# One decoder layer on one core: a projection product cut in three, a transpose moved behind three matmuls, and PSUM bank pairs exchanged

## The chip, the cores and the metric

The kernel runs on one core of a Trainium2 chip. The metric is the device time of one execution in microseconds (us), lower is better. The core has five engines, each with a queue of its own that it works through in order: PE (TensorE, matmuls and transposes), ACT (ScalarE), DVE (VectorE), POOL (GpSimd) and SP (SyncE, which here issues nearly all DMAs). They wait for each other through semaphores.

## The reference, cut to what matters

One layer of a decoder block for 256 tokens of width 1024, all in float32:

```python
z = rmsnorm(x, g_mix) @ w_in                       # 1024 -> 5184 columns
nq, nkv, ngate, dq, dk, dv, iq, ik, iw, ga, gb = split_cols(z, IN_SPLITS)
o_a = nsa_mixer(nq, nkv, ngate, ...)               # compressed, selected and window branch
o_b = dsa_mixer(dq, dk, dv, iq, ik, iw, ...)       # indexer keeps 64 keys of a query
merged = sigmoid(ga) * (o_a @ w_branch_a) + sigmoid(gb) * (o_b @ w_branch_b)
x = x + merged @ w_out
x = x + moe_ffn(rmsnorm(x, g_ffn), ...)            # top 4 of 32 experts, 12 MB of weights each
x = x + sigmoid(rmsnorm(x, g_ple) @ w_ple_gate) * (p @ w_ple)
```

The compressed branch of the first mixer pools windows of 32 raw keys and values:

```python
zb = z[:, cmp_tok] + pe                            # raw keys or values plus a position table
hdn = silu(einsum('bclgd,lde->bcge', zb, w1))
```

## The kernel before, in words

Every engine has a hand-written program. In order of time there are three parts.

**Front.** `ORDER` lists the first stages. `Z0` to `Z6` are the first seven of eleven products of x with a block of columns of `w_in` (`CHUNKS`, at most 512 columns). A product has 8 matmuls (over the 8 row tiles of the weight, `KT`) for each of 2 token tiles `t`. In program text a matmul of float32 is one instruction; in the trace it is two records, so a row with x16 is 8 matmuls. Product c goes to PSUM banks `ps[2*(c%2)+t]`. ACT copies a finished tile into `z` (line 769), scaled by the norm, and counts `z_ev` up; PE counts `z_ps` up when a tile is done. The stages `T:...` are transposes: PE writes one of the banks ps4 and ps5 in turn, ACT copies it out and counts `t_ev`, and the job after next may only start when that bank is copied (`tbank`). `T:K0`, `T:K1` (lines 1286, 1287) are the keys of the selected and the window branch, `T:R0`, `T:R1` (line 1291) the raw keys and values of the compressed branch for each token tile, `T:PE` (line 1295) the position table. After `T:PE` is copied, DVE adds the position table in eight instructions (line 1005, `zb`) and counts `zb_ready`. Product 6 (`Z6`) is the value block of the second mixer, which nothing reads until the first `values` step. POOL adds the mask to the bias (line 667, `Bd`) once `T:R1` is there.

**Attention.** 24 units of two heads (`UNITS`) are worked through in 28 steps. At step u PE does `scores(u)` (line 1372), a special stage if the step has one, `flip(u-3)` (the transposes of the probabilities, line 1380), some matmuls of the four remaining products of `w_in` (`late`, line 1408; 3 a step at first, into banks ps0 and ps1) and `values(u-4)` (lines 1395, 1399). The special stage of step 1 is `HID` (line 1353), the first matmuls of the compressed branch, which wait for `zb_ready`. At step 11 (`C_AFTER`) PE also does `T:C0` and `T:C1` (line 1309), transposes of the compressed branch's probabilities. DVE works on the logits (lines 1065, 1076), ACT does exponentials (783) and copies: probabilities (792), outputs (800), late products (809).

**After attention.** `branch(i)` (line 1439) multiplies the mixers' outputs with `w_branch_a` and `w_branch_b`, two banks for each i. Before `branch(0)` PE waits for `ld_wab`, for all outputs (`o_ev`) and for the copies of all late products (`z_ev`). Then come merged rows, `w_out` (line 1460), the norm, the router and its ranks, and the experts: `visit` for each of 32 experts, with line 369 for the first weights. A visit takes six pieces of 2 MB, in a ring of nine slots.

**DMA.** SP's queue is in order. It loads product c's weights into one of four buffers (`WBUF`) when the product before in this buffer is done (`z_ps`). The first five expert pieces are issued after `o_ev`, two after the fourth `branch` (`pr_ps`), one after `wo_ps` 4, one after `hp_ready`, and each one from then on when PE has used the piece in its slot (`pieces_used`; lines 313 and 315).

Of the kernel before, what the change touches and what calls it, by code (L numbers as in the profile page):

```python
# [18 lines left out]
ALU = mybir.AluOpType  # L19
# [39 lines left out]


ORDER = ["T:G", "T:X0", "T:X1", "T:X2", "T:X3", "Z0", "ER", "Z1", "T:IX0", "T:IX1", "Z2", "I", "T:DQ0", "T:DQ1", "Z3",
         "T:DK0", "T:DK1", "Z4", "T:NQ0", "T:NQ1", "Z5", "Z6", "T:K0", "T:K1", "T:R0", "T:R1", "T:PE"]

UNITS = [("dsa", t, j) for t in (0, 1) for j in range(4)] + [(b, t, j) for t in (0, 1) for j in range(4) for b in ("slc", "win")]
NU = len(UNITS)
# [3 lines left out]
STAGE_AT = {1: "HID", 5: "CMPKV", 7: "T:KC", 8: "T:CS"}  # L69
HIDDEN_AT, KEYS_AT, NORMED_AT, C_SOFT = 3, 5, 6, 9  # L70
C_AFTER = 8


TJOBS = [x for x in ORDER if x.startswith("T:")]
# [24 lines left out]
def block_kernel(nc, io, out):  # L99
    ctx = ExitStack()  # L100
    with ctx:
# [425 lines left out]
        with nc.Block() as block:  # L527
# [160 lines left out]
            def _(sc):  # L688
# [66 lines left out]
                for stage in ORDER:  # L755
                    if stage.startswith("T:"):
                        tjob(stage)
                    elif stage == "ER":
                        sc.wait_ge(er_ps, 1)
                        a.copy(erow, ps[6][0:16, 0:384]).then_inc(er_sb, 1)  # L760
                    elif stage[0] == "Z":
                        c = int(stage[1:])
                        o, n = CHUNKS[c]
                        for t in range(TT):
                            sc.wait_ge(z_ps, 2 * c + t + 1)
                            src = ps[2 * (c % 2) + t][:, 0:n]
                            if c == 0 and t == 0:
                                sc.wait_ge(x_rs, 1)
                            a.activation(z[:, t, o:o + n], src, ACT.Copy, scale=rs[:, t:t + 1]).then_inc(z_ev, 1)
                        if c == C_N2:  # L770
                            sc.wait_ge(z_ev, 2 * c + 2)
                            a.activation(gsig, z[:, :, O_NG:O_NG + 24], ACT.Sigmoid)
                    elif stage == "I":
                        for i in range(6):
                            sc.wait_ge(i_ps, i + 1)
                            if i >= 2:
                                sc.wait_ge(i_used, i - 1)
                            a.activation(rl[:, i % 2, :], ps[7 - i % 2][:, :], ACT.Relu).then_inc(i_rl, 1)
# [124 lines left out]
            def _(ve):  # L903
# [207 lines left out]
                for i in range(4):  # L1111
                    t, n = i // 2, (i % 2) * 512
                    ve.wait_ge(pr_ps, i + 1)
                    ve.wait_ge(gates_ready, t + 1)
                    ch(d.tensor_tensor(mtmp[:, 0, :], ps[2 * (i % 2)][:, :], gates[:, t, n:n + 512], ALU.mult))
                    ch(d.tensor_tensor(mtmp[:, 1, :], ps[2 * (i % 2) + 1][:, :], gates[:, t, DM + n:DM + n + 512], ALU.mult))
                    d.tensor_tensor(merged[:, t, n:n + 512], mtmp[:, 0, :], mtmp[:, 1, :], ALU.add).then_inc(pr_used, 1)
                    ve.wait_ge(pr_used, i + 1)
                ve.wait_ge(ld_consts, 16)
# [14 lines left out]
                def add(i):  # L1134
                    t, c = i // 2, slice((i % 2) * 512, (i % 2 + 1) * 512)
                    ve.wait_ge(wo_ps, i + 1)
                    d.tensor_tensor(x[:, t, c], ps[i][:, :], x[:, t, c], ALU.add).then_inc(x2_ready, 1)

                def square(i):

# [111 lines left out]
            def _(te):  # L1252
# [59 lines left out]
                for stage in ORDER:  # L1312
                    if stage.startswith("T:"):
                        tjob(stage)
                    elif stage[0] == "Z":
                        c = int(stage[1:])
                        o, n = CHUNKS[c]
                        te.wait_ge(ld_w[WBUF[c]], 16 * WBUF[0:c + 1].count(WBUF[c]))
                        if c >= 2:
                            te.wait_ge(z_ev, 2 * (c - 1))  # L1320
                        wv = wbuf[:, WBUF[c] * 4096:WBUF[c] * 4096 + KT * n].rearrange("p (k n) -> p k n", k=KT)
                        for t in range(TT):
                            for k in range(KT):
                                if c == 0 and t == 0 and k % 2 == 0:
                                    te.wait_ge(t_ev, 2 + k // 2)
                                l = mm(ps[2 * (c % 2) + t][:, 0:n], hTv[:, k, t * P:(t + 1) * P], wv[:, k, :], start=k == 0, stop=k == KT - 1)  # L1326
                            l.then_inc(z_ps, 1)
                    elif stage == "ER":
                        te.wait_ge(ld_tab, 48)
                        mm(ps[6][0:16, 0:384], tab, onehot, start=True, stop=True).then_inc(er_ps, 1)  # L1330
# [82 lines left out]
                for u in range(STEPS):  # L1413
# [4 lines left out]
                    if 3 <= u < NU + 3:  # L1418
                        flip(u - 3)
                        if u - 3 == C_AFTER:  # L1420
                            tjob("T:C0")
                            tjob("T:C1")
                    for step in LATE_OF[u]:
                        late(*step)
                    if u >= 4:
                        values(u - 4)


                te.wait_ge(ld_wab, 48)
                te.wait_ge(o_ev, NITEM)  # L1430
                te.wait_ge(z_ev, 2 * NZ)

                def branch(i):
                    t, n = i // 2, (i % 2) * 512
                    if i >= 2:
                        te.wait_ge(pr_used, i - 1)
                    for m_ in range(2):
                        for j in range(4):
                            l = mm(ps[2 * (i % 2) + m_][:, :], oTv[:, m_, j, t * P:(t + 1) * P], (wa, wb)[m_][:, j, n:n + 512], start=j == 0, stop=j == 3)  # L1439
                    l.then_inc(pr_ps, 1)  # L1440

                def half_rows(src, n, at, cols):
# [11 lines left out]
                def w_out(i, ks=range(KT)):  # L1454
# [2 lines left out]
                        te.wait_ge(t_ev, NT + 2 * t + 2)  # L1457
                        te.wait_ge(pr_used, 3 + t)
                    for k in ks:
                        l = mm(ps[i][:, :], hTv[:, k, t * P:(t + 1) * P], wo[:, k, n:n + 512], start=k == 0, stop=k == KT - 1)  # L1460
                    if ks[-1] == KT - 1:
                        l.then_inc(wo_ps, 1)

# [115 lines left out]
```

## Time and profile before

| | |
|---|---|
| time, median of 3 runs (lowest, highest) | 1246.31 us (1244.42, 1247.02) |
| time of the profiled execution | 1244.73 us |
| its span in the trace | 1242.8 us |
| PE busy | 1143.1 us (92%) |
| DVE, ACT, POOL busy | 273.6, 188.1, 35.6 us |
| mean DMA rate | 361 GB/s, 448.29 MB |
| start of `branch(0)` | 219.11 us |
| start of the first expert matmul | 289.64 us |

Times in the trace start at the span's start. A row of an engine gives start, duration and instruction, and in brackets how long the engine stood idle before it and what released it. A matmul's duration holds its way through the array, so the starts of neighbouring rows, and not the sum of durations, tell how long a piece of PE's program takes.

### The profile page before, as it was taken

How to read it: one execution, taken by the hardware profiler on the slowest of the kernel's cores; microseconds unless marked ns; L12 is line 12 of the kernel's file. 1: busy time of each engine (PE TensorE's matmuls, PEld its weight loads, DVE VectorE, ACT ScalarE, POOL GpSimd, SP SyncE). 2: the span in 40 equal slices, each digit the busy share in tenths (PEclk: the TensorE clock that was granted, in tenths of full speed). 3: DMA queues.
4: the chain of work that ended last, by engine and by line, in shares of the span. 5: the costliest groups of instructions: out<-in, count | busy, mean ns of one | idle time of the engine just before them, and what ended most of it. 6: DMA issues, size and time to landing. Idle time of an engine off the chain costs nothing.

```text
span 1242.8 us, 15211 instructions
## 1 busy us (share of the span) xinstructions
PE 1143.1 (92%) x6372; PEld 475.9 (38%) x6372; DVE 273.6 (22%) x786; ACT 188.1 (15%) x405; POOL 35.6 (3%) x49
## 2 busy tenths in 40 slices
PE   7998999998999999998899888888888888888878
PEld 4454544454333343333333333333333333333334
DVE  1473534254111121111111111111111111111122
ACT  2223434222111111111100000000000000000010
POOL 2121100000000000000000000000000000000000
PEclk9999999998999999999999999999999999999999
DMA  8935050969999999999999999999999999999980
GB/s 275 331 136 175 28 136 1 402 234 352 429 426 427 429 428 428 428 429 428 425 426 427 429 428 429 428 428 429 429 428 428 430 429 428 427 429 429 427 341 34
DMA packets 51626, 448.29 MB, mean 361 GB/s; under 512 B 9298, under 2 KB 12215, under 8 KB 26919
## 3 DMA queue, kind: packets, MB, share of 16 engines
q1 hardware_dynamic: 49998, 441.67, 85.8%
q0 software_dynamic: 1264, 5.27, 1.2%
q10 hardware_dynamic: 328, 0.86, 0.3%
q8 instruction: 25, 0.41, 0.1%
q14 instruction: 11, 0.08, 0.0%
HBM read 446.71 MB, written 4.22 MB: 363 GB/s over the span
## 4 chain that ended last, share of the span: by engine, by line
PE 59%; DMA 37%; ACT 2%; DVE 1%; issue 1%; ACTq 0%; POOL 0%; DVEq 0%; POOLq 0%
DMA ring<-in_w_e 24%; PE ps L369 16%; DMA wbuf<-in_w_e 13%; PE ps L396 11%; PE ps L1326 7%; PE ps L1408 4%; PE ps L347 3%; PE ps L338 2%; PE ps L1525 2%; PE ps L1439 2%; PE ps L1460 2%; PE ps L1372 2%; ACT wbuf L460 1%; PE ps L386 1%; PE ps L1399 1%; PE ps L361 1%
## 5 line engine op out<-in xcount | busy, mean ns | idle before, releaser
L369 PE MATMUL ps<-ring,wbuf 128*64 128x512 f32 x1392 | 312.7, 596 | 35.0 <-DMA ring<-in_w_e 34.7
L369 PEld LDWEIGHTS ps<-ring,wbuf 128*64 128x64 f32 x1392 | 96.5, 137 | 238.9 <-issue 162.2
L507 DVE TENSOR_SCALAR oT<-ps 128x512 f32<-128x512 f32 x32 | 22.1, 692 | 737.0 <-PE ps L369 737.0
L369 PE MATMUL ps<-wbuf 128*64 128x512 f32 x656 | 147.8, 595 | 17.5 <-DMA wbuf<-in_w_e 17.4
L396 PE MATMUL ps<-ring,wbuf 128*64 128x512 f32 x672 | 149.5, 595 | 14.2 <-ACT wbuf L460 14.2
L456 ACT ACTIVATE oT<-oT 128x512 f32<-128x512 f32 x32 | 20.1, 630 | 510.5 <-DVE oT L507 510.5
L369 PEld LDWEIGHTS ps<-wbuf 128*64 128x64 f32 x656 | 45.1, 136 | 113.3 <-issue 75.4
L1326 PE MATMUL ps<-wbuf,hT 128*128 128x512 f32 (+2 forms) x224 | 86.5, 545 | 0.0
L396 PEld LDWEIGHTS ps<-ring,wbuf 128*64 128x64 f32 x672 | 46.4, 137 | 102.1 <-issue 83.9
L396 PE MATMUL ps<-wbuf 128*64 128x512 f32 x352 | 78.6, 595 | 7.4 <-ACT wbuf L460 7.4
L347 PE MATMUL ps<-wbuf 64*128 64x512 f32 x264 | 65.6, 615 | 0.7 <-ACT wbuf L462 0.7
L1408 PE MATMUL ps<-wbuf,hT 128*128 128x512 f32 x128 | 59.8, 594 | 0.0
L1326 PEld LDWEIGHTS ps<-wbuf,hT 128*128 128x128 f32 x224 | 42.9, 194 | 40.2 <-issue 37.1
L338 PE MATMUL ps<-misc,gat 128*128 128x64 bf16 x1584 | 53.7, 193 | 1.7 <-DVE gat L1161 1.7
L338 PEld LDWEIGHTS ps<-misc,gat 128*128 128x128 bf16 x1584 | 52.8, 98 | 2.1 <-DVE misc L1196 1.7
L462 ACT COPY wbuf<-ps 128x512 f32<-128x512 f32 x32 | 18.8, 586 | 230.0 <-PE ps L396 230.0
L396 PEld LDWEIGHTS ps<-wbuf 128*64 128x64 f32 x352 | 24.3, 137 | 53.5 <-issue 44.0
L347 PEld LDWEIGHTS ps<-wbuf 64*128 64x128 f32 x264 | 22.7, 186 | 43.1 <-issue 41.5
L487 DVE TENSOR_TENSOR wbuf<-ps,misc 128x512 f32<-128x512 f32 x33 | 22.8, 692 | 28.6 <-PE ps L338 28.6
L1408 PEld LDWEIGHTS ps<-wbuf,hT 128*128 128x128 f32 x128 | 22.3, 190 | 17.5 <-issue 17.4
L1439 PE MATMUL ps<-wbuf,oT 128*128 128x512 f32 x64 | 27.9, 593 | 1.0 <-ACT gat L809 1.0
L1460 PE MATMUL ps<-wbuf,hT 128*128 128x512 f32 x64 | 28.5, 594 | 0.0
(237 smaller groups left out, 762.0 us busy)
## 6 DMA issues: line engine op xcount, KB each, us to landing
ring<-in_w_e SPq DMA_DIRECT2D x129, 2048.0 KB, 38.0
wbuf<-in_w_e SPq DMA_DIRECT2D x63, 2048.0 KB, 38.1
wbuf<-in_w_in SPq DMA_DIRECT2D x9, 2048.0 KB, 9.2
wbuf<-in_w_out SPq DMA_DIRECT2D x1, 4096.0 KB, 14.0
rel_rows_repeated<-rel_rows POOLq DMA_DIRECT2D x1, 3072.0 KB, 19.6
ring<-rel_rows_repeated POOLq DMA_DIRECT2D x1, 2048.0 KB, 12.0
wbuf<-in_w_branch_a SPq DMA_DIRECT2D x2, 1024.0 KB, 10.0
wbuf<-in_w_branch_b SPq DMA_DIRECT2D x1, 2048.0 KB, 17.9
```

Source lines behind the costliest of these rows:

```text
L338: l = mm(O[:, k * SLOTS:(k + 1) * SLOTS], hp[:, q, t, rows_of(k)], S[:, t, :], start=t == 0 and q == 0, stop=t == TT - 1 and q == 2)
L347: l = mm(ps[4 + 2 * t + n][:, :], wST[h, t * P:(t + 1) * P], oe[h, :], start=start, stop=False, skip_group_check=True)
L369: l = mm((G, Lb)[n // 2][(n % 2) * SLOTS:(n % 2 + 1) * SLOTS, :], xeT[:, k, :], slots[at][:, r * 2 * DFF + n * 512:r * 2 * DFF + (n + 1) * ...
L396: l = mm(O[n * SLOTS:(n + 1) * SLOTS, :], actT[:, r, h * SLOTS:(h + 1) * SLOTS], slots[at][:, r * DM + n * 512:r * DM + (n + 1) * 512], st ...
L487: d.tensor_tensor(xeT, ps[2][:, :].rearrange("p (k c) -> p k c", k=KT), bc(gT[:, 16:24], SLOTS), ALU.mult).then_inc(s["xe_ready"], 1)
L507: d.tensor_scalar(gc, ps[0][:, :], LIMIT, None, ALU.min).then_inc(s["gc_ready"], 1)
L1326: l = mm(ps[2 * (c % 2) + t][:, 0:n], hTv[:, k, t * P:(t + 1) * P], wv[:, k, :], start=k == 0, stop=k == KT - 1)
L1372: mm(ps[2 + u % 2][:, 0:2 * n], q[:, j, t * P:(t + 1) * P], k[:, :, 0:n], start=True, stop=True).then_inc(s_ps, 1)
L1408: l = mm(ps[t][:, :], hTv[:, k, t * P:(t + 1) * P], wbuf[:, WBUF[c] * 4096 + k * 512:WBUF[c] * 4096 + (k + 1) * 512], start=k == 0, stop=k ...
L1439: l = mm(ps[2 * (i % 2) + m_][:, :], oTv[:, m_, j, t * P:(t + 1) * P], (wa, wb)[m_][:, j, n:n + 512], start=j == 0, stop=j == 3)
L1460: l = mm(ps[i][:, :], hTv[:, k, t * P:(t + 1) * P], wo[:, k, n:n + 512], start=k == 0, stop=k == KT - 1)
L1525: l = mm(ps[4 + i % 4][:, 0:w_], x3T[:, k, t * P:(t + 1) * P], wple_g[k // 4][:, k % 4, n:n + w_], start=k == 0, stop=k == KT - 1)
```

## The change

`Z6` is cut in three in `ORDER`: token tile 0 whole, then after `T:K0` and `T:K1` the first four matmuls of tile 1, and after `T:PE` its last four. The new function `product` reads these names. `T:C1` moves on PE from directly behind `T:C0` to behind the three late matmuls of its step; ACT's order is unchanged there. The four `branch` products and the four `w_out` products trade the bank pairs ps0, ps1 and ps2, ps3, and the wait for the last late copy moves from `branch(0)` to `branch(1)`.

```diff
 ORDER = [...
-         "T:DK0", "T:DK1", "Z4", "T:NQ0", "T:NQ1", "Z5", "Z6", "T:K0", "T:K1", "T:R0", "T:R1", "T:PE"]
+         "T:DK0", "T:DK1", "Z4", "T:NQ0", "T:NQ1", "Z5", "Z6 0 0:8", "T:K0", "T:K1", "Z6 1 0:4", "T:R0", "T:R1", "T:PE", "Z6 1 4:8"]
+def product(stage):
+    c, *part = stage[1:].split()
+    if not part:
+        return int(c), [(t, range(KT)) for t in range(TT)]
+    lo, hi = (int(k) for k in part[1].split(":"))
+    return int(c), [(int(part[0]), range(lo, hi))]
...
-                        for t in range(TT):
+                        for t in [t for t, ks in parts if ks[-1] == KT - 1]:
                             sc.wait_ge(z_ps, 2 * c + t + 1)
...
-                    ch(d.tensor_tensor(mtmp[:, 0, :], ps[2 * (i % 2)][:, :], gates[:, t, n:n + 512], ALU.mult))
+                    ch(d.tensor_tensor(mtmp[:, 0, :], ps[2 - 2 * (i % 2)][:, :], gates[:, t, n:n + 512], ALU.mult))
-                    d.tensor_tensor(x[:, t, c], ps[i][:, :], x[:, t, c], ALU.add).then_inc(x2_ready, 1)
+                    d.tensor_tensor(x[:, t, c], ps[(i + 2) % 4][:, :], x[:, t, c], ALU.add).then_inc(x2_ready, 1)
...
-                        for t in range(TT):
-                            for k in range(KT):
+                        for t, ks in parts:
+                            for k in ks:
...
                         if u - 3 == C_AFTER:
                             tjob("T:C0")
-                            tjob("T:C1")
                     for step in LATE_OF[u]:
                         late(*step)
+                    if u - 3 == C_AFTER:
+                        tjob("T:C1")
...
                 te.wait_ge(o_ev, NITEM)
-                te.wait_ge(z_ev, 2 * NZ)
                 def branch(i):
                     t, n = i // 2, (i % 2) * 512
+                    if i == 1:
+                        te.wait_ge(z_ev, 2 * NZ)
```

The order of PE's program around product 6, before. `ps` is a PSUM bank, line 1326 a product of `w_in`, 1286 and 1287 `T:K`, 1291 `T:R`, 1295 `T:PE`, 1372 the first scores; an x behind a row counts instructions.

```order
L1326 MATMUL ps<-wbuf,hT 128x512 [waits z_ev,ld_w0]
L1326 MATMUL ps<-wbuf,hT 128x512 x15
L1286 MATMUL ps<-misc,ring 128x128 [waits qn_ready,t_ev]
L1287 MATMUL ps<-misc,ring 128x128
L1286 MATMUL ps<-misc,ring 128x128 [waits qn_ready,t_ev]
L1287 MATMUL ps<-misc,ring 128x128
L1291 MATMUL ps<-misc,ring 128x128 [waits dup_ready,t_ev]
L1291 MATMUL ps<-misc,ring 128x128 x3
L1291 MATMUL ps<-misc,ring 128x128 [waits dup_ready,t_ev]
L1291 MATMUL ps<-misc,ring 128x128 x3
L1295 MATMUL ps<-misc,gat 128x16 [waits ld_small,t_ev]
```

And the same place of the changed kernel, whose lines are numbered 9 higher here.

```order
L1335 MATMUL ps<-wbuf,hT 128x512 x7
L1295 MATMUL ps<-misc,ring 128x128 [waits qn_ready,t_ev]
L1296 MATMUL ps<-misc,ring 128x128
L1295 MATMUL ps<-misc,ring 128x128 [waits qn_ready,t_ev]
L1296 MATMUL ps<-misc,ring 128x128
L1335 MATMUL ps<-wbuf,hT 128x512 [waits z_ev,ld_w0]
L1335 MATMUL ps<-wbuf,hT 128x512 x3
L1300 MATMUL ps<-misc,ring 128x128 [waits dup_ready,t_ev]
L1304 MATMUL ps<-misc,gat 128x16 [waits ld_small,t_ev]
L1304 MATMUL ps<-misc,gat 128x16
L1335 MATMUL ps<-wbuf,hT 128x512 [waits z_ev,ld_w0]
L1335 MATMUL ps<-wbuf,hT 128x512 x3
```

Four matmuls of the product now stand ahead of `T:R0`, and four behind `T:PE`.

PE's program at step 11 before, with bank numbers: 1380 is `flip(8)`, 1309 `T:C0` and `T:C1`, 1408 the late matmuls, 1399 `values(7)`.

```order
L1380 MATMUL ps4<-misc,ring 128x128 [waits s_prob,t_ev]
L1309 MATMUL ps5<-misc,oT 128x128 [waits c_ready,t_ev]
L1309 MATMUL ps5<-misc,oT 128x128
L1309 MATMUL ps4<-misc,oT 128x128 [waits c_ready,t_ev]
L1309 MATMUL ps4<-misc,oT 128x128
L1408 MATMUL ps0<-wbuf,hT 128x512 x3
L1399 MATMUL ps7<-ring 64x128 [waits o_ev,t_ev]
```

The same step of the changed kernel (lines 9 or 10 higher).

```order
L1390 MATMUL ps4<-misc,ring 128x128 [waits s_prob,t_ev]
L1318 MATMUL ps5<-misc,oT 128x128 [waits c_ready,t_ev]
L1318 MATMUL ps5<-misc,oT 128x128
L1418 MATMUL ps0<-wbuf,hT 128x512 x3
L1318 MATMUL ps4<-misc,oT 128x128 [waits c_ready,t_ev]
L1409 MATMUL ps7<-ring 64x128 [waits o_ev,t_ev]
```

Only the transpose into ps4 has moved, behind the three matmuls into ps0.

## Rows read from the trace of the kernel before

**Rows 1.** Busy time in three stretches: us; busy of engines; granted clock, DMA share, GB/s

```profile
119.50:161.50 42.00, 42.00 (x169) 21.28 (x170) 21.84 (x108) 18.20 (x68) 5.96 (x6) 1.00 0.17 52
...
266.80:279.20 12.40, 12.40 (x45) 6.69 (x43) 7.64 (x11) 6.17 (x7) 0.00 (x0) 1.00 0.19 78
...
296.00:1180.00 884.00, 811.54 (x5036) 305.90 (x5034) 133.24 (x310) 84.46 (x140) 0.00 (x0) 1.00 1.01 428
```

**Rows 2.** Waits of PE, 420 to 1175 us: total, times, longest

```profile
PE ps L369 <- DMA ring<-in_w_e: 32.2, 26, 1.2
```

**Rows 3.** SP's queue in order of time, 280 to 420 us

```profile
285.67 8.10 SPq L313 DMA_DIRECT2D ring<-in_w_e  x2
296.87 3.76 SPq L315 DMA_DIRECT2D ring<-in_w_e  x2
```

**Rows 4.** PE in order of time, 84 to 121 us

```profile
106.46 0.27 PE L1286 MATMUL ps<-misc,ring 128*128 128x128 f32 x1
...
108.36 0.66 PE L1291 MATMUL ps<-misc,ring 128*128 128x128 f32 x4 [1.30 <-ACT ring L726]
109.46 0.66 PE L1291 MATMUL ps<-misc,ring 128*128 128x128 f32 x4 [0.44 <-ACT ring L726]
110.07 0.29 PE L1295 MATMUL ps<-misc,gat 16*128 16x16 f32 x2
110.29 0.70 PE L1372 MATMUL ps<-ring 128*128 128x256 f32 x2
...
115.52 3.89 PE L1353 MATMUL ps<-ring,wbuf 128*64 128x30 f32 x64 [1.52 <-issue]
```

**Rows 5.** ACT in order of time, 84 to 120 us

```profile
106.66 0.69 ACT L769 ACTIVATE ring<-ps,misc 128x512 f32<-128x512 f32 x1 [6.18 <-PE ps L1326]
107.25 2.16 ACT L726 COPY ring<-ps 64x128 f32<-64x128 f32 x8
109.43 1.31 ACT L729 COPY ring<-ps 128x512 f32<-128x512 f32 x2
```

**Rows 6.** DVE and POOL in order of time, 84 to 120 us

```profile
97.31 0.76 DVE L994 COPY ring<-ring 128x512 f32<-128x512 f32 x2
...
110.86 4.56 DVE L1005 TENSOR_TENSOR ring<-ring 64x240 f32<-64x240 f32 x8 [12.79 <-ACT ring L731]
...
110.30 1.67 POOL L667 TENSOR_TENSOR ring<-ring 128x256 f32<-128x256 f32 x2 [14.20 <-PE ps L1291]
```

**Rows 7.** Line 1005: durations in ns (least, median, longest), first and last start

```profile
L1005 DVE TENSOR_TENSOR ring<-ring x8: 538/553/967, 110.9 to 114.9; 64x240 f32<-64x240 f32 x8
```

**Rows 8.** Weight loads of w_in, 100 to 140 us: durations, starts, time to landing

```profile
L543 SPq DMA_DIRECT2D wbuf<-in_w_in x3: 368/368/582, 106.7 to 119.4; - x3
...
DMA to landing us min/median/max: 7.8/8.0/14.6
```

**Rows 9.** PE in order of time, 128 to 138 us

```profile
134.61 2.74 PE L1408 MATMUL ps<-wbuf,hT 128*128 128x512 f32 x6
137.28 0.44 PE L1399 MATMUL ps<-ring 128*64 128x128 f32 x4
```

**Rows 10.** PE and ACT in order of time at step 11, 150 to 172 us

```profile
161.80 0.38 PE L1309 MATMUL ps<-misc,oT 128*128 128x128 f32 x2
164.35 0.44 PE L1309 MATMUL ps<-misc,oT 128*128 128x128 f32 x2 [2.17 <-ACT ring L792]
...
167.30 0.66 PE L1399 MATMUL ps<-ring 128*64 128x128 f32 x8
...
163.95 0.35 ACT L792 COPY ring<-ps 128x256 f32<-128x256 f32 x1
```

**Rows 11.** PE and ACT in order of time, 205 to 292 us

```profile
219.11 20.84 PE L1439 MATMUL ps<-wbuf,oT 128*128 128x512 f32 x48 [1.05 <-ACT gat L809]
...
218.11 0.27 ACT L800 COPY oT<-ps 128x128 f32<-128x128 f32 x1 [4.45 <-PE ps L1399]
218.27 0.69 ACT L809 ACTIVATE gat<-ps,misc 128x512 f32<-128x512 f32 x1
```

More of the change, by code:

```diff
@@ L761, in _ @@
                     elif stage[0] == "Z":
-                        c = int(stage[1:])
+                        c, parts = product(stage)
                         o, n = CHUNKS[c]
-                        for t in range(TT):
+                        for t in [t for t, ks in parts if ks[-1] == KT - 1]:
                             sc.wait_ge(z_ps, 2 * c + t + 1)
@@ L1114, in _ @@
                     ve.wait_ge(gates_ready, t + 1)
-                    ch(d.tensor_tensor(mtmp[:, 0, :], ps[2 * (i % 2)][:, :], gates[:, t, n:n + 512], ALU.mult))
-                    ch(d.tensor_tensor(mtmp[:, 1, :], ps[2 * (i % 2) + 1][:, :], gates[:, t, DM + n:DM + n + 512], ALU.mult))
+                    ch(d.tensor_tensor(mtmp[:, 0, :], ps[2 - 2 * (i % 2)][:, :], gates[:, t, n:n + 512], ALU.mult))
+                    ch(d.tensor_tensor(mtmp[:, 1, :], ps[3 - 2 * (i % 2)][:, :], gates[:, t, DM + n:DM + n + 512], ALU.mult))
                     d.tensor_tensor(merged[:, t, n:n + 512], mtmp[:, 0, :], mtmp[:, 1, :], ALU.add).then_inc(pr_used, 1)
@@ L1315, in _ @@
                     elif stage[0] == "Z":
-                        c = int(stage[1:])
+                        c, parts = product(stage)
                         o, n = CHUNKS[c]
@@ L1326, in _ @@
                                 l = mm(ps[2 * (c % 2) + t][:, 0:n], hTv[:, k, t * P:(t + 1) * P], wv[:, k, :], start=k == 0, stop=k == KT - 1)
-                            l.then_inc(z_ps, 1)
+                            if ks[-1] == KT - 1:
+                                l.then_inc(z_ps, 1)
                     elif stage == "ER":
@@ L1438, in branch @@
                         for j in range(4):
-                            l = mm(ps[2 * (i % 2) + m_][:, :], oTv[:, m_, j, t * P:(t + 1) * P], (wa, wb)[m_][:, j, n:n + 512], start=j == 0, stop=j == 3)
+                            l = mm(ps[2 - 2 * (i % 2) + m_][:, :], oTv[:, m_, j, t * P:(t + 1) * P], (wa, wb)[m_][:, j, n:n + 512], start=j == 0, stop=j == 3)
                     l.then_inc(pr_ps, 1)
@@ L1459, in w_out @@
                     for k in ks:
-                        l = mm(ps[i][:, :], hTv[:, k, t * P:(t + 1) * P], wo[:, k, n:n + 512], start=k == 0, stop=k == KT - 1)
+                        l = mm(ps[(i + 2) % 4][:, :], hTv[:, k, t * P:(t + 1) * P], wo[:, k, n:n + 512], start=k == 0, stop=k == KT - 1)
                     if ks[-1] == KT - 1:
```

## The prediction, as it was made before the changed kernel had run

> **What bounds the kernel now.** I read the busy time by stretches first, then the waits of PE, SP's queue, and the timelines of the places that the change touches.
>
> From 296 us to 1180 us the DMA engines are busy at a share of 1.01, at 428 GB/s, and that is 884 us of the span [rows 1]. PE now and then waits there for expert weights, 32.2 us in 26 waits for the ring's slots alone [rows 2]. So for three quarters of its time the kernel is a stream of expert weights, and nothing done in PE's program there would help. But what comes ahead of the stream is not bound by it. From 266.8 us to 279.2 us the DMA engines are nearly idle, at a share of 0.19 [rows 1]: all pieces that have a slot are there, and the next ones are issued when PE's program gets to them. The last ones ahead of the steady stream are issued one by one, at 285.67 us and after, when slots come free [rows 3]; the row that begins at 296.87 us stands for the moment from which a free slot is always filled. Each of these moments is a count that PE's own progress sets. So a microsecond taken out of PE's path ahead of the experts starts the stream a microsecond earlier, and the 884 us behind it are moved as a block. That is the conversion that I use: one to one.
>
> On PE's path ahead of that, PE is busy for all of the 42 us from 119.5 to 161.5 us [rows 1], while DVE has 21.84 us and ACT 18.20 us of work there. In the attention steps PE sets the pace, and a shift ahead of them is carried through. The idle spots of PE are the three that the change goes for: around the transposes ahead of attention [rows 4], at step 11 [rows 10], and at the first branch product [rows 11].
>
> **Part 1, the product in three parts.** No instruction of work is added or removed; sixteen matmul records move. Before, PE goes from product 6 into `T:K0` at 106.46 us and has to wait three times: 1.30 us for ACT before `T:R0` at 108.36 us, 0.44 us before `T:R1` at 109.46 us, and 1.52 us before `HID` at 115.52 us [rows 4]. The reason of the first two is that ACT must first copy product 6's last tile (from 106.66 us), and then the eight copies of the keys, 2.16 us [rows 5]. The third waits for DVE's eight additions, 4.56 us from 110.86 us, which wait for `T:PE`'s copy [rows 6].
>
> I lay out the new order by starts. Three matmuls of a late burst take from 134.61 us to 137.28 us, 2.67 us, of which 0.1 is the transposes' different start; a matmul is 0.86 us and four are 3.43 us [rows 9]. Token tile 1's eight matmuls, 6.87 us, come out from in front of `T:K0`, which so starts at 106.46 - 6.87 = 99.6 us. Its keys need nothing late: DVE's last copy for `T:R` begins at 97.31 us and lasts 0.76 us, and the keys' norm is before it [rows 6]. `T:K0` and `T:K1` are four transposes, 0.44 us (two each 0.22 us, as from 110.07 to 110.29 us for `T:PE`, rows 4). Then the first four matmuls, from 100.1 to 103.5 us. In this time ACT copies tile 0 and the keys: it ended the same work 2.77 us after it had begun (106.66 to 109.43 us, [rows 5]), so from about 99.7 to 102.5 us. `T:R0` finds its bank free at 103.5 us, and `T:R1` follows at 103.9 us. ACT copies `T:R0` after its 0.66 us, from 104.2 us on, for half of 1.31 us, to 104.85 us. `T:PE` needs that bank: it would start at 104.4 us and starts at 104.9 us. This is a new wait, 0.5 us. With 0.22 us for `T:PE` and 3.43 us for the last four matmuls, the first scores start at 108.55 us instead of 110.29 us, so 1.7 us earlier [rows 4].
>
> DVE: `T:R1`'s and `T:PE`'s copies end at about 105.6 us, the additions at 105.7 + 4.56 = 110.2 us. PE reached `HID` at 115.52 - 1.52 = 114.0 us and now does so at 112.3 us. `zb_ready` is then 2 us old, and the wait of 1.52 us is gone. Part 1 gives 1.7 + 1.5 = **3.2 us**. What hides the additions is now the last four matmuls behind `T:PE`: without them PE would reach `HID` 3.4 us sooner, at 108.9 us, and wait 1.3 us for additions that end at 110.2 us either way. Bounds: if `HID` still waited as before, 1.7 us; if the new wait for ACT didn't arise and the transposes' lead times (twice 0.2 us, 0.66 us against 0.44 us) were all gained, 1.30 + 0.44 + 1.52 + 0.4 = 3.7 us.
>
> Queued behind the new wait on PE are only the four matmuls and the scores. On ACT the copy of tile 1 now stands behind `T:PE`'s copy, and nothing that reads it comes before the first `values`. On SP the load of product 8's weights waits for the end of product 6. It was issued at 106.7 us and is now issued at 108.6 us; three such loads landed 7.8 to 14.6 us after issue [rows 8], so by 123.2 us at the latest. Its first reader is the second matmul of the burst that begins at 134.61 us [rows 9], then at about 132.3 us. Nothing is paid.
>
> One rule speaks about the additions. The first of the eight lasts 967 ns and the median is 553 ns [rows 7]; it begins 0.56 us after POOL's two additions of 1.67 us begin [rows 6]. The Trainium skill, page "SBUF — State Buffer", section "SBUF: two separate sides", has the shared port pair of DVE and GpSimd as an exclusive lock, taken for a whole instruction by a DVE operation with two SBUF inputs against a GpSimd one that reads SBUF. The row agrees with such a block of about 0.4 us. POOL's pair now begins after `T:R1`, at about 104.5 us, and still overlaps the start of DVE's at 105.7 us; by the rule the longest delay is one of POOL's instructions, 0.84 us, and `HID` has 2 us to spare. The sum is the same by both.
>
> **Part 2, `T:C1` behind the late matmuls.** `T:C1` needs the bank that ACT empties from 163.95 us for 0.35 us, and waits 2.17 us for it, from after `T:C0` at 161.80 us to 164.35 us [rows 10]. In the new order the late matmuls start at 162.02 us (0.22 us for `T:C0`), `T:C1` at 162.02 + 2.67 = 164.7 us, 0.4 us after its bank is free, and `values(7)` 0.22 us later, at 164.9 us instead of 167.30 us [rows 10]. **2.4 us.** The late matmuls wait for nothing new. Behind the moved transpose on PE stand `values(7)` and the next scores. Bounds: 2.0 us if the bank came free 0.4 us later than it does, 2.5 us with the lead time of the resumed transposes.
>
> **Part 3, the exchanged banks.** `branch(0)` starts at 219.11 us, 1.05 us after PE's last work, released by ACT's late copy of 0.69 us from 218.27 us. ACT's copy of the last output, from 218.11 us for 0.27 us, ends at 218.38 us [rows 11]. A release of 0.15 us as now (218.96 to 219.11 us) starts the product at 218.53 us. **0.6 us.** The wait moved to `branch(1)`, far behind, costs nothing, and the sigmoids have most of a product's time to finish. Bounds: nothing, if PE's writes to one pair of banks were held up by ACT's reading of the other, to 0.7 us.
>
> **Sum.** 3.2 + 2.4 + 0.6 = 6.2 us. The profiled execution took 1244.73 us, so 1238.5 us; it is 1.6 us below the median of the runs, 1246.31 us, which lie between 1244.42 and 1247.02 us. Against the median the same sum gives 1240.1 us, and I predict 1240.1 us. A measurement of this kernel can tell about 0.2%, 2.5 us, from no change.
>
> **The rivals.**
> 1. *Only part of it arrives*: `HID` waits as before and part 3 gives nothing. 1.7 + 2.0 = 3.7 us, 1242.6 us. Against it: DVE's additions have 2 us to spare in my layout. For it: this rests on ACT's short copies falling in line.
> 2. *The stream hides it.* The weights' stream sets the end and does not start earlier, because the loads ahead of it, or the stream's rate, take what PE gives. Then the time stays at 1246.3 us. For it: 884 us at a DMA share of 1.01 [rows 1]. Against it: the 12.4 us at a share of 0.19 before [rows 1], which no earlier load fills. The Trainium skill, page "SBUF — State Buffer", section "A bandwidth-pool intuition that's wrong (but worth ruling out)", says that HBM is almost always the end-to-end bottleneck; by that rule a shorter front would be worth nothing. The trace agrees for the experts and not for the front.
> 3. *Slower: product 8's weights come too late.* Their issue is 1.9 us later, their use 3.2 us earlier. With a landing of 14.6 us [rows 8] there are still 9 us of slack. It costs from the point at which landing takes over 23.7 us, and beats the whole gain only past 30 us; at 33 us the time would be 1249 us. No row comes near that.
>
> **How the numbers follow.** The forecast gets 0.79, with 1238.5 to 1242 us as its own range. Rival 1 gets 0.10, rival 2 gets 0.08, rival 3 gets 0.03. The bounds of the terms add up to 1.7 + 2.0 + 0 = 3.7 us and 3.7 + 2.5 + 0.7 = 6.9 us, so 1242.6 to 1239.4 us. With the runs' own spread of 1.3 us to each side the range is 1238.0 to 1243.8 us; I put it at 1237.8 to 1243.8 us. It leaves out rivals 2 and 3 and some of the tails. Faster by over 0.2%: forecast and nearly all of rival 1, 0.88. Within: 0.09. Slower: 0.03.
>
> **What would show it.** Part 1: `T:R0` and `T:R1` without a wait, a wait of about 0.5 us for ACT at `T:PE`, first scores at 108.5 us, no wait at `HID`, which starts at 112.3 us. Part 2: no idle time at step 11, whose `values` starts near 161.7 us. Part 3: a gap of about 0.5 us before `branch(0)`, which starts near 212.9 us. Stream: the row of 296.87 us near 290.7 us. It is wrong if PE comes to the experts 6 us earlier and the span does not follow, or if a new wait of several microseconds shows up between steps 2 and 24, most likely on ACT or DVE, whose work PE now reaches sooner.

## The result, and the profile after

| | before | changed |
|---|---|---|
| median (lowest, highest), 6 runs each | 1246.01 us (1244.42, 1247.02) | 1236.93 us (1236.00, 1237.74) |
| ratio, 95% interval | | 0.9929 (0.9916 to 0.9942) |
| profiled execution: time, span | 1244.73, 1242.8 us | 1237.17, 1235.2 us |

The change makes the kernel 9.1 us faster by the medians and 7.6 us by the two profiled executions. The forecast was 6.2 us, 1240.1 us, with a range from 1237.8 us: the direction and the parts were right, the size was too small, and the measured time lies 0.9 us below the range.

The first place in the changed kernel, PE in order of time (the line numbers of the changed kernel are 9 to 12 higher than before):

```profile
98.91 0.27 PE L1295 MATMUL ps<-misc,ring 128*128 128x128 f32 x1
...
99.34 3.60 PE L1335 MATMUL ps<-wbuf,hT 128*128 128x512 f32 x8
102.78 1.04 PE L1300 MATMUL ps<-misc,ring 128*128 128x128 f32 x8
104.06 0.29 PE L1304 MATMUL ps<-misc,gat 16*128 16x16 f32 x2 [0.24 <-ACT ring L738]
104.28 3.70 PE L1335 MATMUL ps<-wbuf,hT 128*128 128x512 f32 x8
107.81 0.59 PE L1382 MATMUL ps<-ring 128*128 128x256 f32 x2
...
111.35 3.92 PE L1363 MATMUL ps<-ring,wbuf 128*64 128x30 f32 x64
...
117.87 0.59 PE L1382 MATMUL ps<-ring 128*128 128x256 f32 x2
```

The waits of [rows 4] are gone: none before `T:R0` and `T:R1` (102.78 us), none before `HID` (111.35 us). A new one of 0.24 us for ACT stands before `T:PE`. From `T:K0` to `HID` it was 9.06 us (106.46 to 115.52 us) and is 12.44 us; eight matmuls, 6.87 us, now lie in it, so 5.57 us are left of the 9.06 us, 3.5 us less.

On DVE the additions now begin at 104.61 us and last as long as in [rows 6]:

```profile
104.61 4.56 DVE L1014 TENSOR_TENSOR ring<-ring 64x240 f32<-64x240 f32 x8 [7.23 <-ACT ring L740]
```

Step 11 on PE, and ACT's copy that had to be waited for in [rows 10]:

```profile
157.66 0.38 PE L1318 MATMUL ps<-misc,oT 128*128 128x128 f32 x2
157.87 2.74 PE L1418 MATMUL ps<-wbuf,hT 128*128 128x512 f32 x6
160.45 0.38 PE L1318 MATMUL ps<-misc,oT 128*128 128x128 f32 x2
160.76 0.66 PE L1409 MATMUL ps<-ring 128*64 128x128 f32 x8
...
159.80 0.35 ACT L801 COPY ring<-ps 128x256 f32<-128x256 f32 x1
```

`T:C1` (160.45 us) finds its bank empty since 160.15 us. Then the first branch product, and SP's row that stands for the start of the steady stream:

```profile
211.98 20.84 PE L1451 MATMUL ps<-wbuf,oT 128*128 128x512 f32 x48 [0.46 <-ACT oT L809]
...
289.22 3.76 SPq L324 DMA_DIRECT2D ring<-in_w_e  x2
```

The gap before the product is 0.46 us instead of 1.05 us [rows 11], and it ends with the copy of the output and not with the late copy. The stream's row has moved from 296.87 us [rows 3] to 289.22 us, 7.65 us, and the span has shrunk by 7.6 us.

One more pair of rows is needed, the first rows of PE behind the first product, of the kernel before and of the changed one:

```profile
20.58 0.81 PE L1330 MATMUL ps<-gat 33*16 33x384 f32 x2
```

```profile
19.89 0.82 PE L1340 MATMUL ps<-gat 33*16 33x384 f32 x2
```

0.69 us of the difference is there before anything that was changed. The first records of `Z0` start 0.49 us apart and the later ones 0.25 us; the closer spacing sets in at about 13.5 us in the profile of before and at about 12.3 us in the changed one. The granted clock reads 1.00 in both there, so the rows show the slow start and not its cause. From here on I take the row behind the first product as the zero of PE's path.

### The profile page after: what moved, and what is told of

The parts are those of the page before. It is cut to its first block, busy times and chain, and to the rows that moved or that the text cites. A ratio compares the mean times of both kernels' runs of the same rounds, so it can differ in the third digit from the quotient of the medians.

```text
span 1235.2 us, 15213 instructions
## 1 busy us (share of the span) xinstructions
PE 1141.3 (92%) x6372; PEld 475.5 (38%) x6372; DVE 272.9 (22%) x786; ACT 188.1 (15%) x405; POOL 35.7 (3%) x49
## 4 chain that ended last, share of the span: by engine, by line
PE 59%; DMA 38%; ACT 1%; DVE 1%; issue 0%; ACTq 0%; POOL 0%; DVEq 0%; POOLq 0%
DMA ring<-in_w_e 25%; PE ps L378 16%; DMA wbuf<-in_w_e 13%; PE ps L405 11%; PE ps L1335 7%; PE ps L1418 4%; PE ps L356 3%; PE ps L347 2%; PE ps L1537 2%; PE ps L1451 2%; PE ps L1472 2%; PE ps L1382 2%; ACT wbuf L469 1%; PE ps L395 1%; PE ps L1409 1%; PE ps L370 1%
## 6 DMA issues: line engine op xcount, KB each, us to landing
ring<-rel_rows_repeated POOLq DMA_DIRECT2D x1, 2048.0 KB, 13.5
```

## The experiments

The first question was whether each part gives what the traces say, 3.5, 2.4 and 0.6 us, or whether there is something that the first profile of before does not show. Theory A: the traces say all. Theory B: a stall costs more than its length, because TensorE's clock falls. Theory C: chance at the start of an execution.

**e1, the product in three parts alone.** The changed kernel with the other two parts taken back:

```diff
-         ... "Z5", "Z6", "T:K0", "T:K1", "T:R0", "T:R1", "T:PE"]
+         ... "Z5", "Z6 0 0:8", "T:K0", "T:K1", "Z6 1 0:4", "T:R0", "T:R1", "T:PE", "Z6 1 4:8"]
```

> Only the product in three parts, the rest as before. Theory A (the terms read from the trace): it takes 3.2 to 3.5 us out of PE's path and the span follows one to one, so 3.2 to 3.5 us faster than before; product 6's region without the waits of 1.30, 0.44 and 1.52 us. Theory B (the stalls cost more than their length, because in some executions TensorE's clock falls at them): more than 4.5 us faster, and the three parts do not get their share in the ratio 3.2 to 2.4 to 0.6. Theory C (the profiled pair and the medians differ by chance of the clock at the start and ahead of the experts): as A, with 1 to 2 us of scatter either way.

1240.61 us (1239.70 to 1241.21, 5 runs), before 1244.33 us on that chip (1243.16 to 1246.56, 22 runs); ratio 0.9963 (0.9950 to 0.9976). 3.7 us: near A by the median, but its highest time is 5.4 us below the highest of before, and its lowest only 3.5 us below the lowest.

**e2, the transpose alone.**

```diff
                             tjob("T:C0")
-                            tjob("T:C1")
                     for step in LATE_OF[u]:
                         late(*step)
+                    if u - 3 == C_AFTER:
+                        tjob("T:C1")
```

> Only the second compressed transpose behind the late matmuls. A: 2.4 us faster, wait of 2.17 us at step 11 gone. B: over 3.5 us faster, since this is the longest stall of the three. C: 2.4 us with 1 to 2 us of scatter.

1241.64 us (1240.70 to 1244.67, 11 runs), ratio 0.9980 (0.9971 to 0.9989), 2.7 us. By size it is A. But its trace shows something that no trace had shown before. PE in order of time:

```profile
114.39 4.53 PE L1353 MATMUL ps<-ring,wbuf 128*64 128x30 f32 x64 [1.52 <-issue]
118.86 5.49 PE L1408 MATMUL ps<-wbuf,hT 128*128 128x512 f32 x6
124.14 0.64 PE L1372 MATMUL ps<-ring 128*128 128x256 f32 x2
```

The three late matmuls behind `HID` take 5.28 us and not 2.67 us as in [rows 9]: the granted clock is 0.67 of full at 116 to 120 us and 0.50 at 120 to 124 us, so TensorE goes from 2.4 GHz to 1.2 GHz. From `HID`'s start to the third scores it is 9.75 us; in the profile of before it was 6.50 us.

**e3, the banks alone.**

```diff
-                te.wait_ge(z_ev, 2 * NZ)
                 def branch(i):
+                    if i == 1:
+                        te.wait_ge(z_ev, 2 * NZ)
...
-... ps[2 * (i % 2) + m_][:, :]
+... ps[2 - 2 * (i % 2) + m_][:, :]
```

> Only the exchanged bank pairs and the wait moved to the second branch product. A: 0.6 us faster, the gap of 1.05 us ahead of the first branch product becomes 0.46 us. B: over 1.5 us. C: 0.6 us with 1 to 2 us of scatter, so not told from no change.

1244.66 us (1242.64 to 1246.22, 12 runs), ratio 0.9998 (0.9989 to 1.0007). Not told from no change, as Theory A's 0.6 us would be. The trace has the shorter gap:

```profile
220.19 2.38 PE L1450 MATMUL ps<-wbuf,oT 128*128 128x512 f32 x5 [0.46 <-ACT oT L809]
```

Here too `HID` to the third scores takes 9.75 us (113.94 to 123.69 us).

**e4, the changed kernel again**, in the same rounds.

> The changed kernel once more, timed on the same chip in the same rounds as its three parts. A: 6.2 to 6.5 us faster than before, the sum of the parts. B: 9 us, as measured first, and the parts add up to it. C: between 5 and 9 us, and the traces of the four kernels differ in how long the matmuls of the first product run at half speed and in when the clock returns ahead of the experts.

1236.59 us (1236.38 to 1237.63, 5 runs), ratio 0.9933 (0.9920 to 0.9946): 7.7 us, between A and B. The parts add up to 3.7 + 2.7 - 0.3 = 6.1 us. The whole gives 1.6 us more than the parts together, which is not clear of noise by itself: the intervals of the four ratios are 1.1 to 1.6 us to each side. What is clear is the spread: before, e2 and e3 spread over 3.4, 4.0 and 3.6 us, e1 and e4 over 1.5 and 1.3 us. So the first part takes a spread away as well as its 3.5 us.

The second group asks what lets the clock fall.

**e5, the kernel before again, profiled.**

> The kernel before, profiled again, nothing changed. Theory B2 (the clock falls to 1.2 GHz behind HID in some executions, as in e2 and e3 at 116 to 124 us, and not in others, as in the first profile): its times fall into two groups about 2.2 us apart, 1243.2 to 1244.8 and 1245.7 to 1247, and this profile belongs to one of them by its clock at 116 to 124 us. Theory C (only chance at the start): one group, and the clock at 116 to 124 us says nothing of the time.

1244.01 us (1243.43 to 1246.54, 11 runs). Eight of the eleven times lie below 1244.5 us and three from 1245.35 us up; the profiled one is 1243.43 us, its clock is up, and `HID` to the third scores takes 6.49 us. The two groups show, but the times of 33 executions of before in these rounds (1242.84 to 1246.63 us) leave hardly a gap between them; what tells them apart is the clock of each execution, in the table behind e16.

**e6, one more matmul in the wait at `HID`**, **e7, one more in the wait at `T:R0` as well.** Both take the kernel before.

```diff
                     elif stage == "HID":
+                        te.wait_ge(i_rl, 6)
+                        mm(ps[6][:, :], hTv[:, 0, 0:P], hT[:, 0:512], start=True, stop=True)
                         te.wait_ge(ld_ck, 32)
```

> The kernel before with one more matmul of 128x512 (0.86 us, its result is not used) in the wait of 1.52 us ahead of HID. PE's path keeps its length, since the wait ends when the additions end. B2, if the wait of 1.52 us is what lets the clock fall: the upper group is gone or rarer, the median falls by 0.5 to 1 us, and the lowest time stays at 1243. B2, if HID's own narrow matmuls let it fall, or the waits ahead of T:R0 and T:R1: no change, both groups stay. Theory C: no change.

> As e6, and one more such matmul in the wait of 1.30 us ahead of T:R0. B2: no upper group in any execution, spread of 1.5 us as in e1 and e4, median 1243.5 to 1244.3 us. If two groups stay here, HID's narrow matmuls alone let the clock fall. Theory C: no change against before.

e6: 1243.99 us (1243.25 to 1245.98, 11 runs), two of them above 1245 us. e7: 1244.21 us (1243.38 to 1246.19, 11 runs), five above 1245 us. With a matmul in it, the wait at `HID` still has 0.68 us of idle time, here in e7 and as much in e6:

```profile
114.91 3.89 PE L1358 MATMUL ps<-ring,wbuf 128*64 128x30 f32 x64 [0.68 <-issue]
```

For the case that the idle time makes the fall I had expected the upper group to go in e7, and to go or be rarer in e6. It stayed in both, so the wait ahead of `T:R0` has no part that shows, and shortening the idle time at `HID` this much is not enough. Whether two of eleven are fewer than before's, these runs can't tell.

**e8, later additions in the changed kernel.** Six of the eight additions are made twice, so that `HID` has to wait again.

```diff
+                            if kv or q:
+                                ch(d.tensor_tensor(zb[h, kv, ...], src, pe, ALU.add))
                             l = d.tensor_tensor(zb[h, kv, ...], src, pe, ALU.add)
```

> The changed kernel with six of the eight additions done twice, in a row (3.6 us more on VectorE), so that HID has to wait for zb_ready 1 to 1.5 us again. The path alone gives 1.2 us more than the changed kernel, 1238 us. B2 with the wait at HID as cause: in addition an upper group 2 us higher, so a spread of 3 us and more. B2 with the waits ahead of T:R0 as cause: no upper group.

1241.97 us (1241.37 to 1243.17, 11 runs), ratio to before 0.9983 (0.9974 to 0.9992). The wait is 1.44 us, and the cost against e4 is 5.4 us, from another chip's rounds whose times of before were 0.4 us higher. PE in order of time, and the granted clock (the third number from the right) of two stretches:

```profile
112.26 5.83 PE L1365 MATMUL ps<-ring,wbuf 128*64 128x30 f32 x64 [1.44 <-issue]
118.02 4.06 PE L1420 MATMUL ps<-wbuf,hT 128*128 128x512 f32 x6
121.91 0.60 PE L1384 MATMUL ps<-ring 128*128 128x256 f32 x2
```

```profile
112.00:116.00 4.00, 3.74 (x47) 3.77 (x47) 2.36 (x12) 1.72 (x8) 1.46 (x2) 0.71 1.05 395
116.00:120.00 4.00, 4.00 (x23) 2.90 (x23) 0.00 (x0) 0.21 (x1) 0.00 (x0) 0.50 1.07 385
```

The changed order with only this wait put back has the clock at 1.2 GHz, and 9.65 us from `HID` to the third scores instead of 6.53 us in e4. The trace accounts for 1.5 us of wait and 3.1 us of clock; 0.8 us of the 5.4 us, from other rounds, is not accounted for. So this stall costs some three times its length. There is no second group 2 us higher as I had expected: all eleven times lie in a band of 1.8 us, where the fall puts them, and the mean granted clock of all eleven is 0.993 to 0.996, where it is 0.997 in all eleven executions of the changed kernel.

The third group takes the wait, or the narrow matmuls, out of the kernel before in other ways.

**e9, the late matmuls of step 1 ahead of `HID`; e10, between `HID`'s two halves.**

```diff
+                    if u == 1:
+                        for step in LATE_OF[u]:
+                            late(*step)
                     if u in STAGE_AT:
                         stage_pe(STAGE_AT[u])
...
-                    for step in LATE_OF[u]:
+                    for step in LATE_OF[u] if u != 1 else []:
                         late(*step)
```

> The kernel before with the three late matmuls of step 1 ahead of HID instead of behind it: real work takes the place of the wait of 1.52 us, nothing else is changed. The path alone: 1.5 us faster. If the wait at HID together with HID's narrow matmuls is what lets the clock fall: no execution with the clock down at 112 to 124 us, no upper group, and against the median of before 2.3 to 2.8 us faster. If the waits of 1.30 and 0.44 us ahead of T:R0 and T:R1 have a share in it: an upper group stays, 1.5 us faster.

> The kernel before with the three late matmuls of step 1 between the two halves of HID. The wait of 1.52 us stays and PE's path is as long as before. If the clock falls because the wait and 3.9 us of narrow matmuls stand in one piece: the upper group is gone, median 1243.6 to 1244, lowest time as before. If the wait alone is enough: two groups as before.

e9: 1243.99 us (1242.62 to 1244.44, 11 runs) against 1245.18 us (1242.98 to 1246.87, 23 runs) for before, ratio 0.9991 (0.9982 to 1.0000). e10: 1244.49 us (1243.24 to 1245.56, 11 runs), ratio 0.9994 (0.9985 to 1.0003). e9 has no time above 1244.5 us, where 12 of 23 executions of before lie above 1245 us: with `HID` between dense matmuls the upper group is gone. But the median moved by 1.2 us and not by 2.3. The traces of both show why: the clock now fell at the next stall, at step 11. PE of e9, and the granted clock there (0.66):

```profile
162.41 0.44 PE L1309 MATMUL ps<-misc,oT 128*128 128x128 f32 x2 [2.17 <-ACT ring L792]
162.68 4.44 PE L1408 MATMUL ps<-wbuf,hT 128*128 128x512 f32 x6
167.05 0.66 PE L1399 MATMUL ps<-ring 128*64 128x128 f32 x8
```

```profile
162.00:166.00 4.00, 3.59 (x7) 1.68 (x8) 0.00 (x0) 1.00 (x4) 0.00 (x0) 0.66 1.03 214
```

From `T:C1` to `values(7)` it is 4.64 us where it was 2.95 us in [rows 10]: 1.7 us lost, more than the 1.5 us of wait that e9 saves. In e10 it is 4.46 us (163.19 to 167.65 us), with the clock up at `HID`, in an execution of 1245.37 us; three of its eleven times lie above 1245 us. Its median does not tell it from before. Its clocks do: none of its eleven executions has the mean granted clock of 0.994 that goes with the fall at `HID`, and 11 of 23 of before on that chip have it. The same wait with half of `HID` behind it was not enough for a fall there.

**e11, two more matmuls ahead of the experts, in the changed kernel; e12, the same with `T:PE` ahead of `T:R0`.** These ask whether the one place where the clock is low in every trace is worth something.

```diff
                 router(1, range(4, KT))
+                mm(ps[0][:, :], ident, x[:, 0, 0:512], start=True, stop=True)
                 te.wait_ge(m_ready, 2)
...
+                mm(ps[0][:, :], ident, x[:, 0, 0:512], start=True, stop=True)
                 n_max = expert_pe(te, first)
```

> The changed kernel with two more matmuls of 128x512, whose results are not used, in PE's waits of 1.58 us (ahead of the ranks) and 1.62 us (ahead of the first gather). If the low clock at 276 to 282 us in the changed kernel comes from these waits, it stays at 2.4 GHz, the gather takes 1.6 us instead of 2.7, and the time falls by 1 to 2 us against the changed kernel (1236.6). If the narrow matmuls of router, ranks and gather are enough to let it fall: no change.

> e11, and the transposes of the position table ahead of those of the raw keys, so that the wait of 0.24 us for ScalarE is gone. The path gives 0.2 to 0.4 us more than e11; if e11 gains nothing, this one is 0.2 to 0.4 us faster than the changed kernel, which can't be told from no change in its median.

e11: 1236.90 us (1236.42 to 1237.44, 5 runs), ratio to before 0.9939 (0.9926 to 0.9951). e12: 1237.09 us (1236.00 to 1238.41, 5 runs; a sixth, at 1499.79 us, is left out here and in the table below); ratio 0.9938 (0.9925 to 0.9951). Neither beats the changed kernel: the 1 to 2 us expected for a clock that stays up did not come. In e12's profile the granted clock is 1.00 all the way to the experts, and from the row behind the first product to the branch product it takes 191.74 us instead of 192.09 us, 0.35 us of the 0.2 to 0.4 us expected from the position table. In e11's profile the clock is 0.57 at 274 to 278 us and back at 1.00 for the gather. The gather of e4 and of e11:

```profile
278.07 2.72 PE L347 MATMUL ps<-misc,gat 128*128 128x64 bf16 x48 [1.61 <-DVE gat L1170]
```

```profile
277.47 1.59 PE L347 MATMUL ps<-misc,gat 128*128 128x64 bf16 x48
279.77 0.44 PE L364 MATMUL ps<-misc,wbuf 128*128 128x128 f32 x2 [0.71 <-DVE wbuf L1217]
```

The gather is 1.1 us shorter, and PE then waits 0.71 us for DVE, and again before the first expert: DVE's chain of ranks and weights is what ends there. The first branch product to the stream's row takes 77.38 us in e4 and 77.08 us in e11. That is no gain that can be told: in the traces with the low clock the stretch takes anything from 77.09 us (e2) to 78.08 us (e8).

**e13, e14, e15, the kernel before, three more profiles; e16, e1's kernel once more.**

> The kernel before, one more execution profiled. If the clock's falls make its scatter: either the clock stays up until 280 us and the time is 1243 to 1244.8 us, or it is down for some microseconds at 113 to 124 us and from HID's start to the third scores takes 9.75 us instead of 6.50 and the time is 1245 to 1246.6 us, or it is down at step 11 and from the third scores to the seventh values takes over 47 us instead of 45.3. If they do not: these intervals and the time are not tied.

> As e13: the kernel before, one more execution profiled, to see which of the three kinds it is and whether its time goes with the kind.

> As e13: the kernel before, one more execution profiled, to see which of the three kinds it is and whether its time goes with the kind.

> The kernel of e1 (product in three parts alone) once more, whose wait of 2.17 us at step 11 is still there. If the falls come where PE idles and its work is narrow: never down at HID, and either up all the way (about 1240 us) or down at 160 to 165 us (about 1241.5 us).

e13 took 1244.01 us, e14 1244.02 us, e15 1246.18 us. PE in order of time, e13 and then e15, the same program:

```profile
115.09 3.89 PE L1353 MATMUL ps<-ring,wbuf 128*64 128x30 f32 x64 [1.52 <-issue]
118.91 2.84 PE L1408 MATMUL ps<-wbuf,hT 128*128 128x512 f32 x6
121.58 0.60 PE L1372 MATMUL ps<-ring 128*128 128x256 f32 x2
```

```profile
114.15 4.50 PE L1353 MATMUL ps<-ring,wbuf 128*64 128x30 f32 x64 [1.53 <-issue]
118.59 5.49 PE L1408 MATMUL ps<-wbuf,hT 128*128 128x512 f32 x6
123.87 0.66 PE L1372 MATMUL ps<-ring 128*128 128x256 f32 x2
```

```profile
116.00:120.00 4.00, 4.00 (x37) 3.36 (x37) 0.46 (x1) 0.76 (x5) 0.43 (x1) 0.65 0.61 194
120.00:124.00 4.00, 4.00 (x6) 1.46 (x5) 0.00 (x0) 0.00 (x0) 0.00 (x0) 0.50 0.95 349
```

In e15 the granted clock is 0.65 and 0.50 of full in these eight microseconds, that is 2.4 GHz going over to 1.2 GHz, and `HID` to the third scores takes 9.72 us instead of 6.49 us. Its time is 2.2 us above the other two: 3.2 us from the clock, less 0.9 us by which its start was ahead. Kind and time go together in the one kernel. e16 took 1241.24 us with the clock up at `HID` and at step 11. I had expected about 1240 us for that kind and 1241.5 us for one with the fall at step 11, so its time missed; it does not show that fall for the first part alone.

**The clock of every execution.** Each timed execution in these rounds, profiled or not, has its mean granted clock on record. The profiles say how to read it: 0.997 where the only fall is the one ahead of the experts, 0.994 where the clock fell at `HID` too (e2, e3, e8, e15), 0.996 where it fell at step 11 too (e9, e10); e11 and e12, with a shorter fall or none ahead of the experts, have 0.998 and 1.000. In the kernel before, the clock parts the times without an overlap:

| kernel | executions | clock 0.997 or more | clock 0.993 to 0.996 |
|---|---|---|---|
| before, in the rounds of e1 to e16 | 93 | 55, 1242.84 to 1244.94 us | 38, 1245.08 to 1246.87 us (35 at 0.994, 3 at 0.996) |
| e2 | 11 | 7, 1240.70 to 1242.07 us | 4, 1243.41 to 1244.67 us |
| e3 | 12 | 6, 1242.64 to 1244.16 us | 6, 1245.16 to 1246.22 us |
| e6 and e7 | 22 | 15, up to 1244.58 us | 7, from 1245.53 us |
| e8 | 11 | 0 | 11 |
| e9 | 11 | 0 | 11, all at 0.996 |
| e10 | 11 | 8, up to 1244.60 us | 3, all at 0.996, from 1245.37 us |
| changed, e1, e4, e11, e12, e16 | 27 | 27 | 0 |

The first six executions of before, ahead of e1, have no clock on record, except the profiled one (0.997). The table also says why e3's median does not show its 0.6 us: six of its twelve executions have the fall and seven of before's 22 on that chip. Among those without it, e3's mean is 1243.5 us and before's 1243.9 us.

## Why the prediction was wrong in size

**The step that failed is the sum against the median.** The prediction said that the profiled execution "is 1.6 us below the median of the runs", and "Against the median the same sum gives 1240.1 us". It took the profiled execution of before for a typical one and its distance from the median for noise of 1.3 us to each side. With that, its term for Part 1 put the wait ahead of `HID` at its length, 1.5 us, in every execution, and the clock at nothing. The runs showed that the distance had a cause. The kernel before has two kinds of execution: in one TensorE's clock stays at 2.4 GHz through `HID`, in the other it falls to 1.2 GHz there, which costs 3.2 us of PE's path and, less the start, 2.2 us of the time (e15 against e13 and e14). The profiled one was of the first kind, and of the six that were timed first, four took 1245.7 us or more. The change takes away the wait ahead of `HID`, and with it the second kind: the mean granted clock is 0.997 in all eleven executions of the changed kernel and in all six of e1's, and in none of the six traces of this order without a wait (the changed kernel, e1, e4, e11, e12, e16) does the clock fall there. Putting the wait back brought it back in all eleven (e8). So the change takes 6.4 us off PE's path in each execution, and 3.2 us more in those that would have been of the second kind. The means bear the account out. Of the first six executions of before, four lie in the second group by their times: 6.4 + 4/6 of 3.2 is 8.6 us, and the means differ by 8.8 us (1245.76 against 1236.92 us). In e4's rounds 7 of 22 are of the second kind: 6.4 + 7/22 of 3.2 is 7.5 us, and the means differ by 7.8 us. The medians show 9.1 us where the second kind is the majority, and 7.7 us where a third are of it.

**Point by point.**

- *Part 1, 3.2 us.* 3.5 us: from the row behind the first product to the third scores it is 101.44 us before and 97.98 us after. The layout held to a few tenths: scores at 107.81 us where 108.55 us was forecast, of which 0.69 us is the start; the new wait for ACT was 0.24 us and not 0.5 us; `HID` did not wait. What this term left out is the clock.
- *Part 2, 2.4 us.* 2.39 us: from the third scores to `values(7)` it is 45.28 us before and 42.89 us after. e2 alone gave 2.7 us.
- *Part 3, 0.6 us.* 0.59 us, 51.81 us against 51.22 us from `values(7)` to the branch product.
- *One to one into the span.* Right. From the stream's row to the span's end it is 945.9 us before and 946.0 us after, and within 945.5 to 946.2 us in all eighteen traces. Rival 2, that the stream hides the gain, is refuted by this, and by the result. The sentence named beside it, from the Trainium skill's page "SBUF — State Buffer", section "A bandwidth-pool intuition that's wrong (but worth ruling out)", calls HBM the end-to-end bottleneck in comparison with SBUF; that a shorter front is worth nothing was drawn from it and is not said there, and here the front's 6.4 us arrived in full. The other difference between the profiled executions lies ahead of the experts, 77.76 us against 77.24 us from the branch product to the stream's row; as far as the traces tell this is scatter, since the five profiles of before spread from 77.33 to 77.76 us there, and e4 has 77.38 us. 6.4 + 0.7 + 0.5 = 7.6 us, all of the profiled difference.
- *Product 8's weights.* No wait for them in the changed kernel: rival 3 did not come.
- *Rival 1*, less than the sum, did not come either; what was missing from the list was a rival on the same side with a larger gain. The range had no term for it: its far end, 6.9 us and the runs' spread, was made of waits at their length. (The ends add up to 1238.1 and 1243.9 us and not to 1238.0 and 1243.8 us; nothing hangs on that.)
- *The additions.* The first of the eight again took 959 ns against a median of 552 ns, and again began 0.6 us after POOL's. `HID` had the room for it. No run took POOL's additions away, so that they cause these 0.4 us is not shown.

**What stays open.** The changed kernel's mean, 1236.9 us, is 0.6 us lower than the first kind's, 1243.9 us, less 6.4 us. The fall at step 11 is not the reason: as far as the mean clocks tell, it came in the 3 of the 93 executions of before that have 0.996, and they took 1245.08 to 1245.50 us. The rest is probably a matter of which executions are counted. The second kind is 2.1 us slower by its mean (1246.0 us) though it loses 3.2 us, so it began earlier, as the traces of that kind did; it is missing from the first kind and not from the changed kernel. With 3.2 us taken off the 38 slower executions, the mean of all 93 is 1243.5 us, and less 6.4 us that is 1237.0 us. This is an estimate over several chips and not an experiment. What makes the clock fall in one execution and not in the next stays open, and e6 and e7 do not say how much of the idle time has to be filled.

## What to carry to other kernels

Before a sum made from one profile is put against a median, look at the single times: if they fall into two groups, find out which one the profile is of, by the mean granted clock of each single execution where it is on record, and profile again until both kinds are seen. A stall of PE next to narrow matmuls can cost more than its length, so price it twice, with the clock up and with the clock down, and keep the second price as the far end of the range. Dense work that is to be done anyway, put into such a place, can be worth more than the gap that it fills; here a spare matmul that filled half of the gap was not enough (e6, e7), and with the first stall filled the clock could fall at the next one (e9).

## What the runs showed of the hardware

The same program with the same waits has its clock fall in some executions and not in others, and in the traces it goes with the start. Where the row behind the first product begins at 19.5 us or earlier (e2 19.46, e3 19.02, e15 19.21, e8 19.30), with a wait ahead of `HID`, the clock fell at `HID`; where it begins at 19.6 us or later with such a wait (e5 19.64, e6 19.74, e14 19.77, e7 19.95, e13 20.15, the first profile 20.58) it did not. All ten agree. e11, with 19.35 us and no wait at `HID`, kept its clock, and so did e10 at `HID`, with 19.11 us and dense matmuls between `HID`'s halves. A start that is ahead by 0.9 us thus went with a time that is 2.2 us longer. That the start decides is not shown: by their clocks all eleven executions of e8 had the fall, over times that spread by 1.8 us. The Trainium skill, page "TensorE: Matmul & The Clock Gate", section "HAM oscillation — how this bites in real kernels", tells of PE's clock dropping behind long DMA waits; the trace agrees that the clock drops to half behind a wait of PE, and here a wait of 1.5 us was enough in some executions, with 3.9 us of narrow matmuls (30 columns) behind it.

The falls had two sizes in time lost: 3.1 to 3.25 us at `HID`, 1.7 us (e9) and 1.5 us (e10) at step 11. Ahead of the experts the clock was low for some microseconds in every trace of before and of the change, and taking that away (e12 shows full clock there) was worth nothing that the times or the path show, because another engine ends there. The row of e12:

```profile
280.63 0.44 PE L364 MATMUL ps<-misc,wbuf 128*128 128x128 f32 x2 [0.75 <-DVE wbuf L1217]
```
